# A hybrid decoder layer: three convolutions moved behind the levels of a triangular inverse, and one step of each level moved from VectorE to ScalarE

## The chip, the cores and the metric
One core of a Trainium2 chip runs one launch of the kernel. The metric is the device time in microseconds (us). The engines are TensorE (PE, with its weight loads as PEld), VectorE (DVE), ScalarE (ACT), GpSimd (POOL) and the DMA queues, issued here by SyncE and POOL. Each engine works through its own instructions in order and waits on semaphores for the others.

## The reference
One layer of a decoder trunk over 256 prompt tokens and 8 sample tokens (T = 264 columns), model width 2048, float32. After an RMSNorm one input projection feeds three groups of heads: A (HGRN2 recurrence, 4 heads), B (gated DeltaNet, 8 heads of 128) and C (RG-LRU, 512 channels). An output projection, a SwiGLU feed-forward of width 5632, and norms and residuals follow. What the change touches is group B:

```python
qkv, buf_b_new = causal_dwconv(concat([bq, bk, bv]), buf_b, b_conv_w, None)   # y = w[0]*x[0:L] + w[1]*x[1:] + w[2]*x[2:] + w[3]*x[3:]
qb, kb, vb = split(silu(qkv), 3)
...
A = where(strict, beta_t * (k_t . k_s) * gam, 0)                # per head and chunk of tokens
sol = triangular_solve(eye + A, rhs, lower=True, unit_diagonal=True)
```

## The kernel before
**Chunks and rounds.** All weights stream through four slots as chunks of 512 rows by 256 columns. ACT's `split` rounds a chunk into `w_hi`, DVE's `lo` computes the rest into `w_lo`, and PE's `chunk` multiplies both parts with both parts of the activations, 24 matmuls in all, in two halves of 12. The seven projection rounds (four of kind "b", two of kind "a", one of kind "c") have 16 positions of one chunk each. At position `pos` ACT splits, and DVE makes the rest of, the chunk three positions ahead.

**The mixer beside the stream.** While round r multiplies, each engine also works on the heads projected in round r-1: after each half-chunk PE runs a piece of `b_step` (it counts half positions, `hp` = 2·pos or 2·pos+1), and after its part of the chunk each other engine runs its `b_step(pos)`. So the mixer of B runs in rounds 1 to 4; round 4 itself projects heads of A. The order on each engine is the order of the code; no planner decides it.

**The inverse by levels.** `b_step` inverts I+A by doubling block sizes. The levels l = 2 to 5 run at pos 6 to 9, l = pos-4. Each has two PE products:
- x(l), at hp = 2·pos (L827, L836): eight small matmuls into PSUM bank 4. It needs from DVE the transposed inverse so far (`TMc`, or `TM`) and the masked matrix (`AL`) of its level.
- p(l), at hp = 2·pos+1, half a chunk later (L849): four matmuls, YT times XM, into bank 5. It waits for both operands (semaphore "xc").

Between x and p DVE transposes the first half of x's result out of PSUM (L1876, `YT`), and spreads the second half over the block diagonal of `XM`, by one multiplication with `blk` broadcast, 128x512 (L1877). Then DVE masks AT for the next level (`level_mask`, L1793), waits for p, subtracts it (L1882), and transposes the result (L1885) for the x of the next position. At pos 9 the result is spread instead (L1887) and all of it is transposed (L1890). ACT does nothing for these levels; at pos 6 to 9 it scales four tiles of sample states each (`decay_states`), at pos 7 also four copies for the outer products (`stationary`), and at pos 6 a SiLU of the gate branch. x(6) and x(7), at pos 10 and 11 (L832), are copied by ACT.

**The convolutions.** In a "b" round the projections of q, k and v are ready after pos 3, 7 and 11. ACT copies each into `xraw` (at pos 4, 8 and 12), DVE makes the four taps, two tiles each (`convolve`): q in two parts at pos 6 and 7, k at pos 9 and 10, v at pos 12. ACT's SiLU of each (`silu_conv`) stands at pos 7, 11 and 14, and waits for the convolution to be done. One buffer `conv` serves all three. POOL refills the history columns of `xraw` once a convolution has read them.

Of the kernel before, what the change touches and what calls it, by code (L numbers as in the profile page):

```python
# [30 lines left out]
P = 128  # L31
# [16 lines left out]
CONVW = 4  # L48
XW = 3 + L + NB * CONVW
CW = XW - 3  # L50
B_ROUNDS, A_ROUNDS = 4, 2
# [25 lines left out]
def hybrid_layer(nc, x_prompt, x_sample, state_hgrn, state_gdn, state_gdn_conv, state_rglru_h, state_rglru_conv,  # L77
# [5 lines left out]
    with ExitStack() as ctx:  # L83
# [39 lines left out]
        conv = put("conv", [P, 2, CW])  # L123
# [36 lines left out]
        TMc = sqv[:, 512:640].rearrange("p (x t) -> p x t", x=4)  # L160
        TTc = sqv[:, 640:768].rearrange("p (x t) -> p x t", x=4)
        YT = sqv[:, 768:896].rearrange("p (r t) -> p r t", r=4)
        fold = sqv[:, 768:1024].rearrange("p (x t) -> p x t", x=4)
        kq_st = u[:, :, :].rearrange("p a (c i) -> p (a c) i", i=32)

# [435 lines left out]
        def _(pe):  # L601
# [161 lines left out]
            def b_step(hp, n):  # L763
# [53 lines left out]
                if 12 <= hp <= 23:  # L817
# [21 lines left out]
                    else:  # L839

                        if l < LEVELS - 1:
                            pe.wait_ge(mx["xc"], 10 * n + 2 * l - 2)
                        else:
                            pe.wait_ge(mx["xc"], 10 * n + l + 3)
                        if l == 2:
                            pe.wait_ge(mx["at"], 2 * n + 2)
                        for x in range(4):
# [330 lines left out]
        def _(act):  # L1178
# [88 lines left out]
            def silu_conv(n, which, f=ACT.Silu):  # L1267
                act.wait_ge(conv_done, n + 1)
                A(qkv[:, which, :, 0:L], conv[:, :, 0:L], f).then_inc(silu_done, 1)
                A(qkv[:, which, :, L:T], conv[:, :, L + 3:CW:CONVW], f).then_inc(silu_done, 1)  # L1270

            def evac_plain(g, par, which, f):
                acc_ready(g)
                A(qkv[:, which], acc(par), f).then_inc(drained[par], 1)
# [9 lines left out]
            def decay_states(n, i, factor):  # L1284

                for x in range(4 * i, 4 * i + 4):
                    last = A(Ss[:, x, :], Ss[:, x, :], scale=factor[:, x:x + 1])
                last.then_inc(mx["sdec"], 1)

            def b_step(pos, n):  # L1290
                first = isinstance(n, int) and n == 0
# [111 lines left out]
                    A(S[:, :, 0, :], quad(4)[:, 0:2]).then_inc(mx["s1c"], 1)  # L1403
                finish(pos, n)

            def round_(r, kind, prev, mixer, silu_pos=6):

                for pos in range(SLOTS):
                    slot, turn = (pos + AHEAD) % RING, (pos + AHEAD) // RING
                    if not isinstance(r, int) or SLOTS * r + pos + AHEAD >= RING:  # L1410
                        split(4 * r + turn, slot)
                    q = pos // 4
                    if pos in (4, 8, 12):
                        evac_group(r, kind, q - 1)
                    if prev and pos == silu_pos:
                        act.wait_ge(drained[1], 2 * r)
                        A(qkv[:, 3], qkv[:, 3], ACT.Silu).then_inc(g_done, 1)
                    if kind == "a" and pos == silu_pos:
                        act.wait_ge(drained[0], 2 * r + 1)
                        A(qkv[:, 0], qkv[:, 0], ACT.Silu).then_inc(g_done, 1)  # L1420
                    mixer(pos)
                    if kind == "c" and pos in (13, 15):
                        i = (pos - 13) // 2
                        free_qkv(r, i)
                        silu_conv(12 + i, i, ACT.Copy)
                    if kind == "b" and pos in (7, 11, 14):
                        if not isinstance(r, int) or r > 0:

                            act.wait_ge(mx["nrm"], 2 * r)
                            if pos == 14:  # L1430
                                act.wait_ge(mx["us"], 6 * r)
                        silu_conv(3 * r + q - 1, q - 1)
                    if prev and pos == 1:

                        if not isinstance(r, int) or r > 1:
                            act.wait_ge(mx["og"], 2 * r - 2)
                        evac_plain(4 * r - 1, 1, 3, ACT.Copy)
# [33 lines left out]
                    gating_end()  # L1471

            round_(0, "b", False, mixer0)
            round_(1, "b", True, lambda pos: b_step(pos, 0))
            with act.Fori(2, B_ROUNDS) as r:
                round_(r, "b", True, lambda pos: b_step(pos, r - 1))
            round_(4, "a", True, lambda pos: b_step(pos, 3))
            round_(5, "a", True, lambda pos: a_step(pos, 4, 0), 9)
            round_(6, "c", True, lambda pos: a_step(pos, 5, 1), 9)

# [150 lines left out]
        def _(dve):  # L1631
# [137 lines left out]
                    dve.wait_ge(s, n)  # L1769

            def convolve(n, slot, base, bias=None, taps=range(CONVW)):
                if 0 in taps:
                    dve.wait_ge(raw_q, 2 * n + 2)
                    after(silu_done, 2 * n)
                for j in taps:
                    for t in range(2):
                        w = convw[:, slot, t, j:j + 1]
                        x = xraw[:, slot, t, j:j + CW]
                        if j == 0 and bias is not None:
                            ins = tsc(conv[:, t], x, w, bias[:, t:t + 1], mul, add)  # L1780
                        elif j == 0:
                            ins = tsc(conv[:, t], x, w, None, mul)
                        else:
                            ins = stt(conv[:, t], x, w, conv[:, t], mul, add)  # L1784
                    if j < CONVW - 1:
                        link(ins, base)
                    else:
                        ins.then_inc(conv_done, 1)


            def level_mask(l):

                return tt(AL, AT[:, :, :], masks[:, l, :].unsqueeze(1).broadcast_to([P, 4, P]), mul)  # L1793

            def b_step(pos, n):
                up4 = lambda f: pair[:, f, :].unsqueeze(2).broadcast_to([P, 4, P])
# [73 lines left out]
                    tt(oT[:, :, L:T], j2(small[:, 4, :]), j2(small[:, 5, :]), add).then_inc(mx["os"], 1)  # L1870
                if 6 <= pos <= 9:
                    l = pos - 4
                    by_block = blk[:, :].unsqueeze(1).broadcast_to([P, 4, 4]).unsqueeze(3).broadcast_to([P, 4, 4, 32])
                    wide = lambda a: a.unsqueeze(2).broadcast_to([P, 4, 4, 32])
                    dve.wait_ge(mx["x"], 6 * n + l - 1)
                    dve.transpose(YT, ps[:, 4, 0:P]).then_inc(mx["xc"], 1)  # L1876
                    tt(XM.rearrange("p r (x t) -> p r x t", x=4),  # L1877
                       wide(ps[:, 4, P:2 * P].rearrange("p (r t) -> p r t", r=4)), by_block, mul).then_inc(mx["xc"], 1)
                    if l < LEVELS - 2:
                        level_mask(l + 1).then_inc(mx["al"], 1)  # L1880
                    dve.wait_ge(mx["p"], 6 * n + l - 1)
                    tt(TTc, TTc, ps[:, 5, 0:P].rearrange("p (x t) -> p x t", x=4), sub).then_inc(mx["t"], 1)  # L1882
                    dve.wait_ge(mx["t"], 12 * n + 2 * l - 2)
                    if l < LEVELS - 2:
                        dve.transpose(TMc, TTc).then_inc(mx["t"], 1)  # L1885
                    else:
                        tt(TT[:, :, :].rearrange("p x (r t) -> p x r t", r=4), wide(TTc), by_block, mul)\  # L1887
                            .then_inc(mx["tt"], 1)
                        dve.wait_ge(mx["tt"], 4 * n + 4)
                        dve.transpose(TM, TT[:, :, :]).then_inc(mx["t"], 1)  # L1890
# [151 lines left out]
                        .then_inc(mx["os"], 1)  # L2042

            CV = 3

            def round_(r, kind, mixer, fin, before=lambda pos: None):
                for pos in range(SLOTS):
                    if not isinstance(r, int) or SLOTS * r + pos + AHEAD >= RING:
                        lo(SLOTS * r + pos + AHEAD, (pos + AHEAD) % RING)
                    q = pos // 4  # L2050
                    before(pos)
                    if kind == "b" and pos == 12:
                        chained[0] = 2 * CV
                        convolve(3 * r + 2, 0, 3 * CV * r)
                    mixer(pos)
                    if kind == "c" and pos in (12, 14):
                        i = (pos - 12) // 2
                        chained[0] = CV * i
                        convolve(12 + i, i, 12 * CV, params[:, C_BIAS + 2 * i:C_BIAS + 2 * i + 2])
                    if kind == "b" and pos in (6, 7, 9, 10):  # L2060
                        if pos in (6, 9):
                            chained[0] = CV * (q - 1)
                        convolve(3 * r + q - 1, q - 1, 3 * CV * r,
                                 taps=range(0, 2) if pos in (6, 9) else range(2, CONVW))
                    if pos == 15 and fin is not None:
                        finish(*fin)

# [23 lines left out]

            dve.wait_ge(st_act, 12)
            dve.wait_ge(st_dve, 34)
            round_(1, "b", lambda pos: b_step(pos, 0), (0, 4, B_NORM))
            with dve.Fori(2, B_ROUNDS) as r:
                round_(r, "b", lambda pos: b_step(pos, r - 1), (r - 1, 2 * r + 2, B_NORM))
            round_(4, "a", lambda pos: b_step(pos, 3), (3, 10, B_NORM))
            round_(5, "a", lambda pos: a_step(pos, 4, 0), (4, 0, A_NORM))
            round_(6, "c", lambda pos: a_step(pos, 5, 1), (5, 2, A_NORM))

# [228 lines left out]
```

## Time and profile before
| | |
|---|---|
| median of 3 runs | 1389.5 us (1389.03 to 1390.3) |
| the profiled execution | 1389.01 us, span 1387.3 us |
| PE busy | 1360.2 us, 98% of the span |
| DVE busy | 843.9 us, 61% |
| ACT busy | 678.7 us, 49% |
| mean granted TensorE clock | 0.997 |

Busy time is the union of an engine's instructions. The 1.7 us between the profiled time and the span lie around the first and last instruction. The seven projection rounds lie between about 37 and 500 us of the span, and those with the mixer of B between about 87 and 372 us. The granted clock is a share of full speed.

### The profile page before, as it was taken

What the parts mean: (1) busy time and instruction counts of PE and PEld (TensorE: products, weight loads), DVE (VectorE), ACT (ScalarE), POOL (GpSimd) and SP (SyncE); (2) the same over time, 40 slices, a digit from 0 to 9 for tenths busy, and PEclk for the clock granted to TensorE, in tenths of its full rate; (3) what the DMA queues carried; (4) which work ended last, traced back from release to release, by engine and by line L of the source; (5) the groups of instructions that cost most, each with busy time, mean ns of one, the idle gap of its engine ahead of it and who ended that gap; (6) DMA issues with size and microseconds to landing.
All of it is one profiled execution on the core that took longest, in us unless ns stands there. A gap on an engine that the chain in (4) does not pass through costs nothing.

```text
span 1387.3 us, 28222 instructions
## 1 busy us (share of the span) xinstructions
PE 1360.2 (98%) x11459; PEld 1322.4 (95%) x11459; DVE 843.9 (61%) x1210; ACT 678.7 (49%) x948; POOL 72.2 (5%) x154
## 2 busy tenths in 40 slices
PE   9998989899999999999999999999999999999998
PEld 6997979798999999999999999999999999999998
DVE  5678777878597976476555555555555544444443
ACT  6454646556575685465444444444444434443333
POOL 4010201010201010200000000000000000000000
PEclk9999999999999999999999999999999999999999
DMA  6463635455466446645655555555655555555552
GB/s 211 134 180 95 198 111 152 135 150 165 150 183 194 145 148 205 187 133 160 206 179 182 177 181 179 181 180 181 181 181 181 181 180 180 179 180 180 182 182 79
DMA packets 225255, 234.10 MB, mean 169 GB/s; under 512 B 10443, under 2 KB 220526, under 8 KB 224900
## 3 DMA queue, kind: packets, MB, share of 16 engines
q1 hardware_dynamic: 220500, 218.86, 51.1%
q0 software_dynamic: 4672, 14.04, 3.5%
q8 instruction: 63, 1.03, 0.3%
q14 instruction: 20, 0.16, 0.0%
HBM read 223.45 MB, written 9.65 MB: 168 GB/s over the span
## 4 chain that ended last, share of the span: by engine, by line
PE 87%; DVE 7%; ACT 3%; issue 2%; DMA 1%; SPq 0%; ACTq 0%; POOL 0%; DVEq 0%
PE ps L641 26%; PE ps L642 26%; PE ps L643 26%; DVE w_lo L1638 2%; DVE conv L1784 1%; ACT w_hi L1180 1%; PE ps L941 1%; PE ps L760 1%; DMA xtok<-in_x_prompt_dram 1%; PE ps L770 1%; PE ps L1129 1%; PE ps L667 0%; DVE rs L1877 0%; PE ps L796 0%; PE ps L849 0%
## 5 line engine op out<-in xcount | busy, mean ns | idle before, releaser
L1638 DVE TENSOR_TENSOR w_lo<-raw,w_hi 128x1024 fp32r<-128x1024 f32 x408 | 499.7, 1227 | 434.8 <-ACT w_hi L1180 433.0
L1180 ACT ACTIVATE w_hi<-raw 128x1024 fp32r<-128x1024 f32 x408 | 431.0, 1059 | 554.5 <-PE ps L643 549.0
L641 PE MATMUL ps<-act_hi,w_hi 128*128 128x264 f32 x2296 | 665.6, 290 | 0.7 <-DVE act_lo L1652 0.4
L642 PE MATMUL ps<-act_lo,w_hi 128*128 128x264 f32 x2296 | 652.4, 284 | 0.0
L643 PE MATMUL ps<-act_hi,w_lo 128*128 128x264 f32 x2296 | 651.5, 284 | 0.0
L641 PEld LDWEIGHTS ps<-act_hi,w_hi 128*128 128x128 f32 x2296 | 433.1, 189 | 8.7 <-issue 6.1
L642 PEld LDWEIGHTS ps<-act_lo,w_hi 128*128 128x128 f32 x2296 | 433.6, 189 | 1.2
L643 PEld LDWEIGHTS ps<-act_hi,w_lo 128*128 128x128 f32 x2296 | 432.3, 188 | 0.0
L642 PE MATMUL ps<-hid_lo,w_hi 128*128 128x264 f32 x696 | 197.8, 284 | 0.0
L641 PE MATMUL ps<-hid_hi,w_hi 128*128 128x264 f32 x696 | 197.7, 284 | 0.0
L643 PE MATMUL ps<-hid_hi,w_lo 128*128 128x264 f32 x696 | 197.6, 284 | 0.0
L641 PEld LDWEIGHTS ps<-hid_hi,w_hi 128*128 128x128 f32 x696 | 131.1, 188 | 0.0
L642 PEld LDWEIGHTS ps<-hid_lo,w_hi 128*128 128x128 f32 x696 | 130.9, 188 | 0.0
L643 PEld LDWEIGHTS ps<-hid_hi,w_lo 128*128 128x128 f32 x696 | 130.8, 188 | 0.0
L641 PE MATMUL ps<-cat_hi,w_hi 128*128 128x264 f32 x248 | 70.9, 286 | 0.0
L643 PE MATMUL ps<-cat_hi,w_lo 128*128 128x264 f32 x248 | 70.3, 284 | 0.0
L642 PE MATMUL ps<-cat_lo,w_hi 128*128 128x264 f32 x248 | 70.3, 283 | 0.0
L642 PEld LDWEIGHTS ps<-cat_lo,w_hi 128*128 128x128 f32 x248 | 46.7, 188 | 0.1
L641 PEld LDWEIGHTS ps<-cat_hi,w_hi 128*128 128x128 f32 x248 | 46.7, 188 | 0.1
L643 PEld LDWEIGHTS ps<-cat_hi,w_lo 128*128 128x128 f32 x248 | 46.6, 188 | 0.0
L1784 DVE SCALAR_TENSOR_TENSOR conv<-xraw,convw,conv 128x288 f32<-128x288 f32 x84 | 39.7, 514 | 1.2
L535 POOL DMA_DIRECT2D out_dram<-Ss x12 | 10.7, 894 | 250.0 <-DVE S L2038 100.2
(386 smaller groups left out, 1064.6 us busy)
## 6 DMA issues: line engine op xcount, KB each, us to landing
raw<-in_w_in_dram SPq DMA_DIRECT2D x112, 512.0 KB, 3.7
raw<-in_w_gate_dram SPq DMA_DIRECT2D x88, 512.0 KB, 3.5
raw<-in_w_up_dram SPq DMA_DIRECT2D x88, 512.0 KB, 3.5
raw<-in_w_down_dram SPq DMA_DIRECT2D x88, 512.0 KB, 4.4
raw<-in_w_out_dram SPq DMA_DIRECT2D x32, 512.0 KB, 3.5
out_dram<-Ss POOLq DMA_DIRECT2D x12, 512.0 KB, 5.2
Ss<-in_state_gdn_dram POOLq DMA_DIRECT2D x8, 512.0 KB, 6.6
xtok<-in_x_prompt_dram SPq DMA_DIRECT2D x2, 1024.0 KB, 6.0
```

The costliest lines, as they stand in the source:

```text
L535: pool.dma_start(dst_s[0, :, ds(2 * k + j, 1)].rearrange("b o d e -> d (b o) e"), Ss[:, 8 * j:8 * j + 8, :]).then_inc(mx["st"], 16)
L641: pe.matmul(out, wh, x_hi[:, kk], start=(kk == begin), stop=False)
L642: pe.matmul(out, wh, x_lo[:, kk], start=False, stop=False)
L643: last = pe.matmul(out, wl, x_hi[:, kk], start=False, stop=(kk == nk - 1))
L760: pe.matmul(ps[:, 7 - a * (g % 2), :], k_st[a][:, g, :], u_mv[a][:, :, :], start=True, stop=True)\
L770: last = pe.matmul(ps[:, 4 + i, 0:T], ones[:, :], sq[:, i], start=True, stop=True)
L941: last = pe.matmul(ps[:, 4 + l // 4, (l % 4) * P:(l % 4) * P + P], w, w, start=True, stop=True)
L1129: ins = pe.matmul(ps[:, Y_BANKS[q][t], k * P:k * P + P], src[:, 4 * q + k, t * P:t * P + P], ident, is_transpose=True, start=(first and k ...
L1180: return act.activation(out, in_, f, **kw)
L1638: tt(w_lo[:, slot], raw[:, slot], w_hi[:, slot].bitcast(F32), sub).then_inc(lo_done, 1)
L1784: ins = stt(conv[:, t], x, w, conv[:, t], mul, add)
```

## The change
1. DVE's two steps between x(l) and p(l) at pos 6 to 9 are replaced. ACT copies the first half of x's result to SBUF (`Yc`), and spreads the second half by four copies of 128x128, each scaled by one column of `blk`. DVE transposes `YT` out of `Yc`.
2. Both parts are called by `ahead(pos)`, first thing at a position: ahead of ACT's `split` and DVE's `lo` of the chunk three ahead. Before, DVE's part came behind its `lo`.
3. The first tap of the three convolutions of a "b" round goes to ACT (`first_tap`: two scaled copies of 128x288), at pos 4 for q, and behind the SiLU of the one before it at pos 11 and 12 for k and v.
4. DVE's other three taps go to pos 10, 11 and 12, one convolution each. ACT's SiLUs go to pos 11, 12 and 14.
5. Semaphore counts follow: "xc" counts three steps per level, `raw_q` three per convolution of B. The convolutions of C keep their four taps on DVE.

```diff
 # TensorE
-  pe.wait_ge(mx["xc"], 10 * n + 2 * l - 2)
+  pe.wait_ge(mx["xc"], 14 * n + 3 * l - 3)
 # ScalarE
+            def first_tap(n, slot):
+                act.wait_ge(raw_q, 3 * n + 2)
+                if not isinstance(n, int) or n > 0:
+                    act.wait_ge(silu_done, 2 * n)
+                for t in range(2):
+                    last = A(conv[:, t], xraw[:, slot, t, 0:CW], scale=convw[:, slot, t, 0:1])
+                last.then_inc(raw_q, 1)
...
+            def b_answer(pos, n):
+                if 6 <= pos <= 9:
+                    if pos == 6:
+                        act.wait_ge(mx["ks"], n + 1)
+                    act.wait_ge(mx["x"], 6 * n + pos - 5)
+                    A(Yc, ps[:, 4, 0:P]).then_inc(mx["xc"], 1)
+                    for x in range(4):
+                        last = A(XM[:, :, 32 * x:32 * x + 32], ps[:, 4, P:2 * P].rearrange("p (r t) -> p r t", r=4),
+                                 scale=blk[:, x:x + 1])
+                    last.then_inc(mx["xc"], 1)
...
                 for pos in range(SLOTS):
+                    ahead(pos)
                     slot, turn = (pos + AHEAD) % RING, (pos + AHEAD) // RING
...
-                    if kind == "b" and pos in (7, 11, 14):
+                    if kind == "b" and pos == 4:
+                        first_tap(3 * r, 0)
+                    if kind == "b" and pos in (11, 12, 14):
+                        i = (11, 12, 14).index(pos)
...
-                        silu_conv(3 * r + q - 1, q - 1)
+                        silu_conv(3 * r + i, i)
+                        if i < 2:
+                            first_tap(3 * r + i + 1, (i + 1) % 2)
 # VectorE
+            def b_answer(pos, n):
+                if 6 <= pos <= 9:
+                    dve.wait_ge(mx["xc"], 14 * n + 3 * pos - 17)
+                    dve.transpose(YT, Yc).then_inc(mx["xc"], 1)
...
                 if 6 <= pos <= 9:
                     l = pos - 4
-                    dve.wait_ge(mx["x"], 6 * n + l - 1)
-                    dve.transpose(YT, ps[:, 4, 0:P]).then_inc(mx["xc"], 1)
-                    tt(XM.rearrange("p r (x t) -> p r x t", x=4),
-                       wide(ps[:, 4, P:2 * P].rearrange("p (r t) -> p r t", r=4)), by_block, mul).then_inc(mx["xc"], 1)
                     if l < LEVELS - 2:
+                        dve.wait_ge(mx["x"], 6 * n + l - 1)
                         level_mask(l + 1).then_inc(mx["al"], 1)
...
                 for pos in range(SLOTS):
+                    ahead(pos)
                     if not isinstance(r, int) or SLOTS * r + pos + AHEAD >= RING:
                         lo(SLOTS * r + pos + AHEAD, (pos + AHEAD) % RING)
                     q = pos // 4
                     before(pos)
-                    if kind == "b" and pos == 12:
-                        chained[0] = 2 * CV
-                        convolve(3 * r + 2, 0, 3 * CV * r)
                     mixer(pos)
...
-                    if kind == "b" and pos in (6, 7, 9, 10):
-                        if pos in (6, 9):
-                            chained[0] = CV * (q - 1)
-                        convolve(3 * r + q - 1, q - 1, 3 * CV * r,
-                                 taps=range(0, 2) if pos in (6, 9) else range(2, CONVW))
+                    if kind == "b" and pos in (10, 11, 12):
+                        i = pos - 10
+                        chained[0] = TAPS * i
+                        convolve(3 * r + i, i % 2, 3 * TAPS * r, taps=range(1, CONVW))
```

## Rows read from the trace of the kernel before
**Rows 1.** TensorE's waits: line, released by, us in total, times, longest.
```profile
PE ps L849 <- DVE rs L1877: 13.2, 10, 2.9
PE ps L985 <- DVE gz L1684: 1.2, 1, 1.2
```
**Rows 2.** Timeline of TensorE, round 4: start us, us, engine, line, operation, count.
```profile
333.02 0.43 PE L827 MATMUL ps<-sq 128*32 128x128 f32 x8
333.26 0.40 PE L836 MATMUL ps<-masks,sq 128*32 128x128 f32 x8
...
342.62 0.43 PE L827 MATMUL ps<-sq 128*32 128x128 f32 x8
...
345.07 0.43 PE L849 MATMUL ps<-rs,sq 128*32 128x128 f32 x8
347.09 0.43 PE L827 MATMUL ps<-sq 128*32 128x128 f32 x8
...
351.86 0.44 PE L832 MATMUL ps<-rs,AT 32*32 32x32 f32 x16 [0.23 <-DVE rs L1890]
```
**Rows 3.** Timeline of TensorE, round 1.
```profile
111.96 0.42 PE L827 MATMUL ps<-sq 128*32 128x128 f32 x8
...
127.37 0.66 PE L849 MATMUL ps<-rs,sq 128*32 128x128 f32 x8 [2.93 <-DVE rs L1877]
130.82 0.42 PE L827 MATMUL ps<-sq 128*32 128x128 f32 x8
...
135.59 0.44 PE L832 MATMUL ps<-rs,AT 32*32 32x32 f32 x16 [0.23 <-DVE rs L1890]
```
**Rows 4.** Busy time in one us of round 1; PEclk is the granted clock.
```profile
128.00:129.00 1.00, 1.00 (x8) 1.00 (x5) 0.87 (x3) 1.00 (x4) 0.00 (x0) 0.50 0.82 240
```
**Rows 5.** Timeline of TensorE, round 3.
```profile
260.30 0.43 PE L827 MATMUL ps<-sq 128*32 128x128 f32 x8
...
282.52 0.44 PE L832 MATMUL ps<-rs,AT 32*32 32x32 f32 x16 [0.23 <-DVE rs L1890]
```
**Rows 6.** Timeline of ScalarE, round 2, pos 7.
```profile
197.73 0.75 ACT L1180 ACTIVATE qkv<-conv 128x512 f32<-128x512 f32 x2 [3.05 <-DVE conv L1784]
```
**Rows 7.** Timeline of VectorE, round 2, pos 8.
```profile
199.46 1.22 DVE L1638 TENSOR_TENSOR w_lo<-raw,w_hi 128x1024 fp32r<-128x1024 f32 x1 [1.76 <-ACT w_hi L1180]
200.60 0.31 DVE L1876 STREAM_TRANSPOSE sq<-ps 128x128 f32<-128x128 f32 x1
...
201.41 0.67 DVE L1793 TENSOR_TENSOR sq<-AT,masks 128x512 f32<-128x512 f32 x1
202.04 0.29 DVE L1882 TENSOR_TENSOR sq<-sq,ps 128x128 f32<-128x128 f32 x1
202.36 0.31 DVE L1885 STREAM_TRANSPOSE sq<-sq 128x128 f32<-128x128 f32 x1
```
**Rows 8.** Timeline of ScalarE, round 4, pos 6 and 7.
```profile
332.15 1.28 ACT L1180 ACT_TABLE_LOAD   x1
333.44 1.18 ACT L1180 ACTIVATE qkv<-qkv 128x528 f32<-128x528 f32 x2
...
335.70 1.04 ACT L1180 ACTIVATE w_hi<-raw 128x1024 fp32r<-128x1024 f32 x1
339.26 1.14 ACT L1180 ACTIVATE kst_b<-ps,group 128x128 fp32r<-128x128 f32 x4 [2.52 <-PE ps L749]
340.27 1.28 ACT L1180 ACTIVATE Ss<-Ss,spair 128x128 f32<-128x128 f32 x4
```
**Rows 9.** Timeline of VectorE, round 4, pos 9.
```profile
350.36 0.69 DVE L1887 TENSOR_TENSOR TT<-sq,blk 128x512 f32<-128x512 f32 x1
351.09 0.71 DVE L1890 STREAM_TRANSPOSE rs<-TT 128x512 f32<-128x512 f32 x1
```
**Rows 10.** Round 3, pos 12: TensorE, then VectorE.
```profile
291.82 0.60 PE L871 MATMUL ps<-vb,TT 128*128 128x128 f32 x4
...
293.20 2.92 DVE L1784 SCALAR_TENSOR_TENSOR conv<-xraw,convw,conv 128x288 f32<-128x288 f32 x6
```

More of the change, by code:

```diff
@@ L162, in hybrid_layer @@
         YT = sqv[:, 768:896].rearrange("p (r t) -> p r t", r=4)
+        Yc = sqv[:, 896:1024]
         fold = sqv[:, 768:1024].rearrange("p (x t) -> p x t", x=4)
@@ L841, in b_step @@
                         if l < LEVELS - 1:
-                            pe.wait_ge(mx["xc"], 10 * n + 2 * l - 2)
+                            pe.wait_ge(mx["xc"], 14 * n + 3 * l - 3)
                         else:
-                            pe.wait_ge(mx["xc"], 10 * n + l + 3)
+                            pe.wait_ge(mx["xc"], 14 * n + l + 7)
                         if l == 2:
@@ L1404, in a_step, with round_ @@
                 finish(pos, n)
-            def round_(r, kind, prev, mixer, silu_pos=6):
+            def round_(r, kind, prev, mixer, silu_pos=6, ahead=lambda pos: None):
                 for pos in range(SLOTS):
+                    ahead(pos)
                     slot, turn = (pos + AHEAD) % RING, (pos + AHEAD) // RING
@@ L1425, in round_ @@
                         silu_conv(12 + i, i, ACT.Copy)
-                    if kind == "b" and pos in (7, 11, 14):
+                    if kind == "b" and pos == 4:
+                        first_tap(3 * r, 0)
+                    if kind == "b" and pos in (11, 12, 14):
+                        i = (11, 12, 14).index(pos)
                         if not isinstance(r, int) or r > 0:
                             act.wait_ge(mx["nrm"], 2 * r)
-                            if pos == 14:
+                            if i == 2:
                                 act.wait_ge(mx["us"], 6 * r)
-                        silu_conv(3 * r + q - 1, q - 1)
+                        silu_conv(3 * r + i, i)
+                        if i < 2:
+                            first_tap(3 * r + i + 1, (i + 1) % 2)
                     if prev and pos == 1:
@@ L1473, in _ @@
             round_(0, "b", False, mixer0)
-            round_(1, "b", True, lambda pos: b_step(pos, 0))
+            round_(1, "b", True, lambda pos: b_step(pos, 0), ahead=lambda pos: b_answer(pos, 0))
             with act.Fori(2, B_ROUNDS) as r:
-                round_(r, "b", True, lambda pos: b_step(pos, r - 1))
-            round_(4, "a", True, lambda pos: b_step(pos, 3))
+                round_(r, "b", True, lambda pos: b_step(pos, r - 1), ahead=lambda pos: b_answer(pos, r - 1))
+            round_(4, "a", True, lambda pos: b_step(pos, 3), ahead=lambda pos: b_answer(pos, 3))
             round_(5, "a", True, lambda pos: a_step(pos, 4, 0), 9)
@@ L1771, in convolve @@
             def convolve(n, slot, base, bias=None, taps=range(CONVW)):
-                if 0 in taps:
-                    dve.wait_ge(raw_q, 2 * n + 2)
-                    after(silu_done, 2 * n)
+                if bias is None:
+                    dve.wait_ge(raw_q, 3 * n + 3)
+                else:
+                    dve.wait_ge(raw_q, 2 * n + 2 + 3 * B_ROUNDS)
+                    dve.wait_ge(silu_done, 2 * n)
                 for j in taps:
@@ L1778, in convolve @@
                         x = xraw[:, slot, t, j:j + CW]
-                        if j == 0 and bias is not None:
+                        if j == 0:
                             ins = tsc(conv[:, t], x, w, bias[:, t:t + 1], mul, add)
-                        elif j == 0:
-                            ins = tsc(conv[:, t], x, w, None, mul)
                         else:
@@ L1793, in level_mask, with wide @@
                 return tt(AL, AT[:, :, :], masks[:, l, :].unsqueeze(1).broadcast_to([P, 4, P]), mul)
+            by_block = blk[:, :].unsqueeze(1).broadcast_to([P, 4, 4]).unsqueeze(3).broadcast_to([P, 4, 4, 32])
+            def wide(a):
+                return a.unsqueeze(2).broadcast_to([P, 4, 4, 32])
+            def b_answer(pos, n):
+                if 6 <= pos <= 9:
+                    dve.wait_ge(mx["xc"], 14 * n + 3 * pos - 17)
+                    dve.transpose(YT, Yc).then_inc(mx["xc"], 1)
             def b_step(pos, n):
@@ L1872, in b_step @@
                     l = pos - 4
-                    by_block = blk[:, :].unsqueeze(1).broadcast_to([P, 4, 4]).unsqueeze(3).broadcast_to([P, 4, 4, 32])
-                    wide = lambda a: a.unsqueeze(2).broadcast_to([P, 4, 4, 32])
-                    dve.wait_ge(mx["x"], 6 * n + l - 1)
-                    dve.transpose(YT, ps[:, 4, 0:P]).then_inc(mx["xc"], 1)
-                    tt(XM.rearrange("p r (x t) -> p r x t", x=4),
-                       wide(ps[:, 4, P:2 * P].rearrange("p (r t) -> p r t", r=4)), by_block, mul).then_inc(mx["xc"], 1)
                     if l < LEVELS - 2:
+                        dve.wait_ge(mx["x"], 6 * n + l - 1)
                         level_mask(l + 1).then_inc(mx["al"], 1)
@@ L2044, in _, with round_ @@
             CV = 3
-            def round_(r, kind, mixer, fin, before=lambda pos: None):
+            TAPS = 2
+            def round_(r, kind, mixer, fin, before=lambda pos: None, ahead=lambda pos: None):
                 for pos in range(SLOTS):
+                    ahead(pos)
                     if not isinstance(r, int) or SLOTS * r + pos + AHEAD >= RING:
@@ L2058, in round_ @@
                         chained[0] = CV * i
-                        convolve(12 + i, i, 12 * CV, params[:, C_BIAS + 2 * i:C_BIAS + 2 * i + 2])
-                    if kind == "b" and pos in (6, 7, 9, 10):
-                        if pos in (6, 9):
-                            chained[0] = CV * (q - 1)
-                        convolve(3 * r + q - 1, q - 1, 3 * CV * r,
-                                 taps=range(0, 2) if pos in (6, 9) else range(2, CONVW))
+                        convolve(12 + i, i, 3 * B_ROUNDS * TAPS, params[:, C_BIAS + 2 * i:C_BIAS + 2 * i + 2])
+                    if kind == "b" and pos in (10, 11, 12):
+                        i = pos - 10
+                        chained[0] = TAPS * i
+                        convolve(3 * r + i, i % 2, 3 * TAPS * r, taps=range(1, CONVW))
                     if pos == 15 and fin is not None:
@@ L2093, in _ @@
             dve.wait_ge(st_dve, 34)
-            round_(1, "b", lambda pos: b_step(pos, 0), (0, 4, B_NORM))
+            round_(1, "b", lambda pos: b_step(pos, 0), (0, 4, B_NORM), ahead=lambda pos: b_answer(pos, 0))
             with dve.Fori(2, B_ROUNDS) as r:
-                round_(r, "b", lambda pos: b_step(pos, r - 1), (r - 1, 2 * r + 2, B_NORM))
-            round_(4, "a", lambda pos: b_step(pos, 3), (3, 10, B_NORM))
+                round_(r, "b", lambda pos: b_step(pos, r - 1), (r - 1, 2 * r + 2, B_NORM),
+                       ahead=lambda pos: b_answer(pos, r - 1))
+            round_(4, "a", lambda pos: b_step(pos, 3), (3, 10, B_NORM), ahead=lambda pos: b_answer(pos, 3))
             round_(5, "a", lambda pos: a_step(pos, 4, 0), (4, 0, A_NORM))
```

## The prediction, made before the result was known
> **What bounds the kernel now.** I read the busy shares first: PE works 98% of the span, so a change that takes nothing from PE can win only PE's idle time, some 27 us, and PE's stretches at a low clock. The view of waits comes second. It says who ends that idle time [rows 1]: 13.2 us in ten waits, all of them p(l) waiting for DVE's spreading multiplication, and one of 1.2 us in round 0 for the small tables at pos 12. Third comes the timeline, to see what stands in front of the late multiplication. In round 2 the long one (2.9 us) is a chain over two engines. ACT's SiLU at pos 7 waits 3.05 us for the first convolution [rows 6], the split of pos 8 is queued behind the SiLU, DVE sits 1.76 us until that split is done [rows 7], and only behind its `lo` may it answer x(4). Rounds 1 and 3 have the same; round 4, without convolutions, has not.
>
> A measure that holds all these waits is the time from x(2), at pos 6, to x(6), at pos 10. It is 18.84 us in round 4 [rows 2], 23.63 in round 1 [rows 3], 22.22 in round 3 [rows 5]; round 2 repeats round 1 with 23.70. Sum 88.39 us. Where PE isn't held it does a position in 4.47 us (342.62 to 347.09 [rows 2]), and the last one in 4.77 - 0.23 = 4.54, so PE's own pace would be about 3 x 4.47 + 4.54 = 17.95.
>
> The extra of round 1 has a second part. Behind the 2.93 us of idle time the granted clock is 0.50, the lower of the two levels, 1.2 GHz [rows 4], and p(4) to x(5) takes 3.45 us [rows 3] where the same work took 2.02 in round 4 [rows 2]. That costs 1.43 us. Round 2 repeats it; round 3 has a wait as long and keeps its clock.
>
> **The new loop.** The answers themselves come in time. x lasts 0.64 us (333.02 to 333.66 [rows 2]). ACT starts some 0.04 later and issues five instructions. The nearest row is `stationary`: four scaled 128x128 copies out of PSUM, 1.01 us from the first's start to the next group's [rows 8], 0.25 each. So the split can start at 0.68 + 1.26 = 1.94 us after x's start, and XM is done 0.13 later, at 2.07. PE reaches p at about 2.0 at pos 6 and 2.45 at pos 7 to 9 (342.62 to 345.07 [rows 2]; there the outer products stand between). The 13.2 us of waits in front of p are gone, but for 0.1 at pos 6.
>
> What is late next? The next x needs DVE's mask, subtraction and transposition, and in DVE's queue they stand behind `lo`, which needs ACT's split, which now stands behind the answers, which need this x. That closes a loop from x to x, which PE can't run ahead of:
> - x ends and ACT starts: 0.68
> - five copies: 1.26, so 1.94
> - split: 1.04 [rows 8], 2.98; DVE's `lo` starts at 3.01
> - `lo` to the next DVE instruction: 1.14 [rows 7], 4.15
> - mask: 0.63, 4.78; subtraction: 0.32, 5.10; transposition: 0.31, 5.41 [rows 7]
> - PE starts the next x 0.06 later: 5.47.
>
> (The p that the subtraction needs ended at 2.5 to 2.9.) At pos 9 there is no mask; subtraction 0.32, spreading 0.73 (350.36 to 351.09), transposition 0.71 [rows 9] give 4.15 + 1.76 + 0.06 = 5.97. From x(2) to x(6): 3 x 5.47 + 5.97 = 22.38 us. PE is held 1.0 us in front of x at pos 8 and 9, and 1.4 at pos 7 and 10.
>
> Is ACT back in time? At pos 6 of rounds 1 to 3, after the split: table load 1.29, then a SiLU and four decays, 2.26 less one SiLU of 0.54 (333.44 to 335.70 [rows 8]), so free at 2.98 + 0.02 + 1.29 + 1.72 = 6.01, against 6.15 when the next x ends. In round 4 there are two SiLUs: 6.55, 0.4 late, so 22.78. At the other positions ACT has over 0.9 us to spare.
>
> **The sum.** Round 1: 22.38 - 23.63 = -1.25. Round 2: -1.32. Round 3: +0.16. Round 4: 22.78 - 18.84 = +3.94. In these the convolutions' stalls and both stretches of low clock are already taken out.
>
> **The convolutions.** In round 0 less stands ahead of the small tables: DVE has spent six tap instructions there (2.92 us [rows 10]) instead of sixteen, and the wait of 1.2 [rows 1] goes: -1.2. In rounds 1 to 3 I put the convolutions' new places at nothing. The first starts about 4.6 us after x(6), when DVE has updated states, and ends at 7.5; `lo` and the subtraction of p(7) follow and end at 9.1, and PE wants that at 9.30 (282.52 to 291.82 [rows 5, 10]). The cover there is only 0.2 us. The second runs from 9.6 to 12.5 and the third from 14.0 to 17.0. Each has six tap instructions of 2.92 in all. The `lo` between them are for chunks that PE starts after 21. On ACT a SiLU and a first tap (no row has its shape; it lies between a 128-column copy, 0.25, and a 528-column one, 0.54, twice; I take 0.75) stand ahead of the copies of u, which then start at 10.8 instead of 10.4, with PE coming for them at 11.6. The first tap at pos 4 falls where ACT idles. POOL's refill follows the first convolution, in time for the copy of v at about 10. If a cover fails, it costs 0.2 to 0.5 us in each of three rounds; if the work in front goes quicker than I think, nothing is won, as PE is not waiting there. Raw loads hang on `lo`, which is four positions ahead of its need.
>
> **Total:** -1.2 - 1.25 - 1.32 + 0.16 + 3.94 = +0.3 us on the profiled execution's 1389.01. The median shown is 0.5 above that one, so I forecast 1389.8.
>
> **The unknown prices.** The five copies are on the loop, sixteen times. Their lower end is the 0.25 above. The upper end is the four decay copies, out of SBUF: 1.28 wide against 1.14 [rows 8], 0.05 more apiece. That gives 16 x 5 x 0.05 = +3.8, 1393.6. I take 0.25, since source and scale are those of `stationary`. The other price is the clock: nothing to win, and at most 1.43 a round.
>
> The Trainium skill, "ScalarE: Activation LUTs", section "Rules for kernel authors", budgets about 0.3 us for an ACTIVATE plus 0.83 ns for each element, and sends multiplications to VectorE. An estimate by it is 0.41 us a copy, 2.0 us for an answer, and some +13 us in all. The trace doesn't agree: four such copies are through in 1.14 us [rows 8]. I leave that rule at a chance of 2%.
>
> **Rivals.**
> 1. *The waits go and nothing takes their place* (10%). For it: all the PE waits that the profile names are for the removed instruction. Against it: two queues in fixed order. Then each round runs at 17.95: 88.39 - 71.8 = 16.6, and 1.2 of round 0: 1371.
> 2. *The clock falls in every round* (18%), at pos 7 to 10, each time PE is held for 1 to 1.4 us. It decides from the point where such short idle times, four in a row, are enough; the rows show a fall only behind 2.9 us, and not behind the 1.2 in round 0. Price: 4 x 1.43 = +5.7, 1395.5. Slower. The Trainium skill, "TensorE: Matmul & The Clock Gate", section "A second HAM failure mode: psum-queue depth-cycling", says that frequent short idles between groups of matmuls can make the clock swing. No row here shows such a swing behind a short idle.
> 3. *The copies are dearer than `stationary`'s* (15%), by the SBUF price: 1393.6. Slower.
> 4. *Half the loop isn't there* (9%), say because ACT's instructions overlap better or PE's first wait is shorter: 0.5 us less in each of the 16 beats minus what PE itself needs, some -5: 1384.
> 5. *The covers of pos 11 and 12 fail* (5%): 3 x 0.5, 1391.3.
>
> The forecast, with its own range 1388 to 1392, has the remaining 41%, after 2% for the rule on ScalarE.
>
> **How the numbers follow.** The range of 1384.5 to 1396 leaves out rival 1, part of rival 4, and the skill's rule. A measurement of this kernel can tell 0.2%, 2.8 us, from no change. Faster by more than that (below 1386.7): rivals 1 and 4 and a little of the forecast, 0.21. Slower (above 1392.3): rivals 2 and 3, the rule, and a tail of the forecast, 0.35. Within: 0.44.
>
> **What would show it.** In the profile after: no wait of L849 over 0.2 us; a new group of PE waits at the first matmuls of x, released by DVE's transpositions, of 1.0 to 1.5 us, about 16 of them; x to x of 5.5 us at pos 6 to 8, and 6.0 from pos 9; on DVE, `lo` at pos 6 to 9 released by ACT's w_hi each time; round 4 longer from x(2) to x(6) by 4 us, rounds 1 and 2 shorter by 1.3; granted clock 1.00 throughout them; the wait in round 0 gone. I am wrong if x starts at PE's own pace of 4.5 us a position (then 1371), or if the clock shows 0.50 in round 4.

## The result and the profile after

The changed kernel takes 1393.78 us (median of 8 runs, 1393.42 to 1395.07) against 1389.14 for the kernel before (8 runs, 1387.54 to 1390.45). The ratio is 1.0034, 95% interval 1.0023 to 1.0045: slower by 4.6 us. The profiled execution took 1393.59 us, its span is 1391.8, 4.5 more than before. Times here and below are medians; one execution of the second experiment's kernel took 3298.8 us at a full granted clock, against 1375.23 to 1375.42 in its other three, and no run shows why.

TensorE's waits after, in the columns of [rows 1]:

```profile
PE ps L828 <- DVE sq L1918: 13.3, 12, 1.3
PE ps L833 <- DVE rs L1923: 5.6, 4, 1.4
...
PE ps L642 <- DVE xT L1725: 0.9, 1, 0.9
```

The waits in front of p (L849 before, L850 here) are gone, and the one for the small tables too. In their place stand twelve waits in front of x(3), x(4) and x(5) (L828) and four in front of x(6) (L833), 18.9 us where there were 13.2 in front of p and 0.9 in front of x(6), all released by DVE's transpositions. (The third row is PE at the start of round 1, waiting for DVE's copy of the residual out of PSUM.) Round 4 on TensorE, which answers to [rows 2]:

```profile
332.19 0.42 PE L828 MATMUL ps<-sq 128*32 128x128 f32 x8
...
337.77 0.43 PE L828 MATMUL ps<-sq 128*32 128x128 f32 x8 [1.27 <-DVE sq L1918]
...
343.55 0.43 PE L828 MATMUL ps<-sq 128*32 128x128 f32 x8 [1.31 <-DVE sq L1918]
...
349.06 0.43 PE L828 MATMUL ps<-sq 128*32 128x128 f32 x8 [0.98 <-DVE sq L1918]
...
355.00 0.44 PE L833 MATMUL ps<-rs,AT 32*32 32x32 f32 x16 [1.39 <-DVE rs L1923]
...
361.07 0.68 PE L833 MATMUL ps<-rs,AT 64*64 64x64 f32 x8
```

And one turn of the loop, from the x at 343.55, first on ScalarE, then on VectorE (to be held against [rows 7, 8]):

```profile
344.25 0.28 ACT L1181 ACTIVATE sq<-ps 128x128 f32<-128x128 f32 x1 [1.06 <-PE ps L837]
344.43 1.14 ACT L1181 ACTIVATE rs<-ps,blk 128x128 f32<-128x128 f32 x4
345.43 1.08 ACT L1181 ACTIVATE w_hi<-raw 128x1024 fp32r<-128x1024 f32 x1
```
```profile
346.55 1.23 DVE L1665 TENSOR_TENSOR w_lo<-raw,w_hi 128x1024 fp32r<-128x1024 f32 x1 [1.67 <-ACT w_hi L1181]
347.69 0.69 DVE L1820 TENSOR_TENSOR sq<-AT,masks 128x512 f32<-128x512 f32 x1
348.29 0.28 DVE L1915 TENSOR_TENSOR sq<-sq,ps 128x128 f32<-128x128 f32 x1
348.61 0.31 DVE L1918 STREAM_TRANSPOSE sq<-sq 128x128 f32<-128x128 f32 x1
```

The reader can follow it by start times: ACT's answers, the split queued behind them, DVE idle until the split is done, then `lo`, mask, subtraction, transposition, and PE's next x at 349.06, 5.51 us after the last.

A second thing shows only in the windows. Busy time and granted clock (third number from the end) behind the wait at pos 10, in rounds 3 and 4:

```profile
282.00:283.00 1.00, 1.00 (x6) 1.00 (x6) 0.00 (x0) 0.00 (x0) 0.00 (x0) 0.50 0.33 27
357.00:358.00 1.00, 1.00 (x7) 1.00 (x6) 0.00 (x0) 0.00 (x0) 0.00 (x0) 0.50 0.37 41
```

The two low stretches of rounds 1 and 2 [rows 4] have gone, and two came in rounds 3 and 4. x(6) to x(7) takes 6.07 us in round 4 above (355.00 to 361.07), 6.09 in round 3, and 4.65 in rounds 1 and 2: some 1.4 us more each. Yet in rounds 1 and 2 PE waits in front of x(6) just as long (1.41 and 1.39 us) and its granted clock stays at 1.00. Round 1:

```profile
133.65 0.44 PE L833 MATMUL ps<-rs,AT 32*32 32x32 f32 x16 [1.41 <-DVE rs L1923]
...
138.30 0.68 PE L833 MATMUL ps<-rs,AT 64*64 64x64 f32 x8
```

The whole difference of the spans by stretches (x(2) to x(6) from the starts of x, rows as above in each round):

| stretch | before | after | difference |
|---|---|---|---|
| to x(2) of round 1 | 111.96 | 111.11 | -0.85 |
| round 1, x(2) to x(6) | 23.63 | 22.54 | -1.09 |
| round 2 | 23.70 | 22.48 | -1.22 |
| round 3 | 22.22 | 22.49 | +0.27 |
| round 4 | 18.84 | 22.81 | +3.97 |
| between rounds 1, 2 and 3 | 101.01 | 101.42 | +0.41 |
| round 3, x(6), to round 4, x(2) | 50.50 | 52.15 | +1.65 |
| behind x(6) of round 4 | 1035.44 | 1036.80 | +1.36 |
| sum | 1387.3 | 1391.8 | +4.5 |

### The profile page after: what moved, and what is told of

Its sections match the earlier page's. It is cut to its first block, busy times and chain, and to the rows that moved or that the text cites. A ratio compares the mean times of both kernels' runs of the same rounds, so it can differ in the third digit from the quotient of the medians.

```text
span 1391.8 us, 28299 instructions
## 1 busy us (share of the span) xinstructions
PE 1360.7 (98%) x11459; PEld 1323.2 (95%) x11459; DVE 827.8 (59%) x1170; ACT 707.5 (51%) x1051; POOL 74.7 (5%) x154
## 4 chain that ended last, share of the span: by engine, by line
PE 87%; DVE 6%; ACT 5%; issue 2%; DMA 1%; SPq 0%; ACTq 0%; DVEq 0%
PE ps L642 26%; PE ps L643 26%; PE ps L644 26%; ACT w_hi L1181 2%; DVE w_lo L1665 2%; ACT rs L1181 1%; PE ps L942 1%; DVE conv L1811 1%; PE ps L771 1%; DVE sq L1820 1%; DMA xtok<-in_x_prompt_dram 1%; PE ps L1130 1%; PE ps L828 0%; PE ps L668 0%; PE ps L761 0%
## 5 line engine op out<-in xcount | busy, mean ns | idle before, releaser
L514 POOL COPY xraw<-hist_b 128x24 f32<-128x24 f32 (+1 forms) x24 | 11.1, 461 | 216.2 <-DVE conv L1811 197.4
```

Source lines behind the costliest of these rows:

```text
L514: pool.tensor_copy(dst[:, :, 0:3], src).then_inc(hist_in, 1)
```

## The experiments

All were run beside the kernel before, which took 1390.05 us beside kernels 1 to 4, 1390.01 beside 5 to 8 and 1389.37 beside 9. Ratios are against it.

**1. Both engines' order turned back.** The question is whether the order closes the loop.

```diff
 # ScalarE, round_
-                    ahead(pos)
                     slot, turn = ...
                         split(4 * r + turn, slot)
+                    ahead(pos)
 # VectorE, round_
-                    ahead(pos)
                         lo(SLOTS * r + pos + AHEAD, (pos + AHEAD) % RING)
+                    ahead(pos)
```

> The changed kernel, but ACT's split and DVE's w_lo of the chunk three ahead stand in front of the answers again. Theory (a loop from x to x through answers, split and w_lo of the same position): the loop opens, x(2) to x(6) falls from 22.5 to 22.8 us to about 18.5 in each of four rounds (some wait of up to 1.4 us stays in front of p at pos 7, where ACT is late by the table load, SiLU and split), the clock stays at 1.00, and the time is 1393.8 - 16.3 - 2.9 = 1374.6 us. Rival (ACT's added load itself is what holds PE, 5 copies a level wherever they stand): x to x stays at 5.5 us and the time within 2 us of 1393.8.

Measured: 1376.67 us (1376.43 to 1377.11), ratio 0.9906 (0.9889 to 0.9922). x(2) to x(6) takes 18.9 us in rounds 1 to 3 and 19.5 in round 4, and no low clock shows in these rounds. That is 2.1 us more than expected: PE still waits in front of p, eight times and 4.0 us in all, for DVE's transposition, which stands behind `lo`. The same instructions in another order are 17.1 us faster than the changed kernel, so ACT's added load isn't what holds PE.

**2. Only ACT's order turned.** The first half of the diff above.

> The changed kernel, only ACT's order turned: split first, then the answers; DVE still transposes before its w_lo. Theory: the split is the one link that closes the loop, so this is as good as both turned, 1374.6 us, within 1 us. Rival (DVE's order matters too): only part of the gain, 1380 or more.

Measured: 1375.33 us, ratio 0.9895 (0.9875 to 0.9914). The split's place on ACT is the link. It is even 1.3 us better than both turned. DVE in round 4, from x(2) at 318.99, shows why the `lo` is harmless now:

```profile
320.09 0.30 DVE L1831 STREAM_TRANSPOSE sq<-sq 128x128 f32<-128x128 f32 x1
320.32 1.18 DVE L1665 TENSOR_TENSOR w_lo<-raw,w_hi 128x1024 fp32r<-128x1024 f32 x1
321.43 0.68 DVE L1820 TENSOR_TENSOR sq<-AT,masks 128x512 f32<-128x512 f32 x1
```

It starts right behind the transposition, 1.33 us after x, with nothing to wait for. What is left is one wait a round, at pos 7, in front of p(3), and ACT shows its cause in round 4:

```profile
321.10 1.28 ACT L1181 ACT_TABLE_LOAD   x1
322.39 1.18 ACT L1181 ACTIVATE qkv<-qkv 128x528 f32<-128x528 f32 x2
323.48 1.27 ACT L1181 ACTIVATE Ss<-Ss,spair 128x128 f32<-128x128 f32 x4
324.64 1.05 ACT L1181 ACTIVATE w_hi<-raw 128x1024 fp32r<-128x1024 f32 x1
325.59 0.26 ACT L1181 ACTIVATE sq<-ps 128x128 f32<-128x128 f32 x1
```
```profile
326.92 0.43 PE L850 MATMUL ps<-rs,sq 128*32 128x128 f32 x8 [1.22 <-ACT rs L1181]
```

**3. Only DVE's order turned.** The second half of the diff.

> The changed kernel, only DVE's order turned: w_lo first, then the transposition of Yc. Theory: DVE's w_lo waits for ACT's split, which waits for x, so YT comes at x + 4.4 us instead of x + 1.3, p waits 2 us for it, and x to x becomes 6.5 us (6.75 from pos 9): 26.2 us from x(2) to x(6), +3.7 a round, 1408.5 us. Rival (the DVE order is harmless): 1394.

Measured: 1411.78 us, ratio 1.016 (1.0143 to 1.0177). x to x is 6.5 us, as expected, and 6.8 from pos 9, but 8.0 from x(2) to x(3); a round takes 27.9. PE waits in front of p now, and DVE of round 2 shows the transposition behind a `lo` that itself waits:

```profile
PE ps L850 <- DVE sq L1831: 32.8, 16, 2.3
```
```profile
201.10 1.22 DVE L1665 TENSOR_TENSOR w_lo<-raw,w_hi 128x1024 fp32r<-128x1024 f32 x1 [5.18 <-ACT w_hi L1181]
202.25 0.30 DVE L1831 STREAM_TRANSPOSE sq<-sq 128x128 f32<-128x128 f32 x1
```

The 1.5 us too many from x(2) to x(3) are low clock. It falls in each of the four rounds behind the first wait in front of p, of 2.20 to 2.26 us, and not behind the twelve waits of 1.95 to 2.03 us that follow. TensorE in round 2, and the granted clock (third number from the end) behind its first and its second wait:

```profile
194.58 0.66 PE L850 MATMUL ps<-rs,sq 128*32 128x128 f32 x8 [2.20 <-DVE sq L1831]
198.10 0.43 PE L828 MATMUL ps<-sq 128*32 128x128 f32 x8
202.60 0.42 PE L850 MATMUL ps<-rs,sq 128*32 128x128 f32 x8 [2.02 <-DVE sq L1831]
```
```profile
195.00:196.00 1.00, 1.00 (x11) 0.83 (x5) 0.70 (x3) 1.00 (x5) 0.00 (x0) 0.50 0.44 55
203.00:204.00 1.00, 1.00 (x12) 1.00 (x9) 0.96 (x4) 0.26 (x1) 0.00 (x0) 1.00 0.44 56
```

That makes four falls where the changed kernel has two, and 1408.5 plus two more of 1.5 us is 1411.5. While ACT answers first, DVE's place for the transposition is worth 18 us; with ACT's split in front (1, 2) it is worth 1.3. So the change's `ahead` on DVE is right; the one on ACT is wrong.

**4. The convolutions' half alone.** Two steps of DVE between x and p as in the kernel before (L1876, L1877), no answers on ACT; first taps, convolutions and SiLUs as in the change; the semaphore counts follow.

```diff
-                        dve.wait_ge(mx["x"], 6 * n + l - 1)
+                    dve.wait_ge(mx["x"], 6 * n + l - 1)
+                    dve.transpose(YT, ps[:, 4, 0:P]).then_inc(mx["xc"], 1)
+                    tt(XM..., wide(ps[:, 4, P:2 * P]...), by_block, mul).then_inc(mx["xc"], 1)
```

> The convolution half of the change alone: first taps on ACT, convolutions at pos 10 to 12, SiLUs at pos 11, 12 and 14; the spreading stays one multiplication on DVE, behind w_lo, as in the kernel before. Theory: the long stall at pos 8 goes, rounds 1 to 3 look like round 4 did before (18.84 us from x(2) to x(6)), no fall of the clock: 1389.1 - 13.0 - 0.85 + 0.4 = 1375.7 us. Rival (the convolutions' new places cost something at pos 10 to 12, or the stall isn't from them): above 1380.

Measured: 1376.04 us, ratio 0.99 (0.9883 to 0.9916). x(2) to x(6) is 18.84 to 18.86 us in all four rounds, exactly what round 4 had before. One wait a round is left in front of p(2), 0.9 us. DVE of round 4 has two `lo` to do before it may answer x(2):

```profile
PE ps L850 <- DVE rs L1897: 3.6, 4, 0.9
```
```profile
320.22 2.35 DVE L1654 TENSOR_TENSOR w_lo<-raw,w_hi 128x1024 fp32r<-128x1024 f32 x2
322.49 0.31 DVE L1896 STREAM_TRANSPOSE sq<-ps 128x128 f32<-128x128 f32 x1
322.72 0.65 DVE L1897 TENSOR_TENSOR rs<-ps,blk 128x512 f32<-128x512 f32 x1
```

**5. The answers' half alone.** All taps on DVE at their old places, SiLUs at pos 7, 11 and 14; `ahead` as in the change.

```diff
-                    if kind == "b" and pos == 4:
-                        first_tap(3 * r, 0)
-                    if kind == "b" and pos in (11, 12, 14):
+                    if kind == "b" and pos in (7, 11, 14):
...
-                    if kind == "b" and pos in (10, 11, 12):
...
+                    if kind == "b" and pos in (6, 7, 9, 10):
...
```

> The other half of the change alone: ACT's answers in front of everything at pos 6 to 9, the convolutions with all taps on DVE at their old places, SiLUs at pos 7, 11 and 14. Theory (the loop of 5.5 us, plus the convolution's stall once a round: the SiLU at pos 7 waits for the convolution until some 2.4 us after the next x, and the answer is queued behind it): x(2) to x(6) of about 24.9 us in rounds 1 to 3 and 22.8 in round 4, so 1389.1 + (97.5 - 88.4) - (2.9 of old low clock already within) = 1398 to 1402 us. Rival (the answers are a gain that the moved convolutions spoil): below 1389.

Measured: 1400.22 us, ratio 1.0071 (1.0054 to 1.0088). x(2) to x(6): 24.91, 24.71, 24.73 and 22.83. Its waits are the loop's, plus three in front of p:

```profile
PE ps L828 <- DVE sq L1913: 13.1, 11, 1.4
PE ps L833 <- DVE rs L1918: 5.6, 4, 1.4
PE ps L850 <- ACT rs L1181: 5.4, 3, 1.8
```

Here too each round has a wait of 1.41 or 1.42 us in front of x(6), and the clock falls behind it in rounds 1 and 4 and not in 2 and 3. It also falls once behind a wait of 1.83 us in front of p(4) in round 1, and not behind those of 1.78 and 1.77 in rounds 2 and 3.

By itself one half is worth -14.0 us (4) and the other +10.2 (5); together they should give -3.8 and gave +4.6. They don't add: without the answers, moving the convolutions wins 14.0 us, and with them (5 against the changed kernel) 6.4, because the loop then holds PE anyway.

**6. A dose on the loop.** The decays, 1.17 us of ACT, between answers and split.

```diff
                                  scale=blk[:, x:x + 1])
                     last.then_inc(mx["xc"], 1)
...
+                    decay_states(n, pos - 6, spair[:, 0, :])
...
-                if 6 <= pos <= 9:
...
-                    decay_states(n, pos - 6, spair[:, 0, :])
```

> The changed kernel, with ACT's four decays of sample states (1.17 us) between the answers and the split instead of behind it: the same work, put on the loop. Theory: each x to x at pos 6 to 9 grows by 1.17, 16 of them, 18.7 us, less 0.4 in round 4 where ACT was late anyway: 1412 us. Rival (ACT's load counts, not its place): 1394.

Measured: 1412.84 us, 19.1 above the changed kernel; ratio 1.0162 (1.0145 to 1.0179). PE's waits in front of x grow from 18.9 to 31.0 us:

```profile
PE ps L828 <- DVE sq L1916: 22.8, 12, 2.4
PE ps L833 <- DVE rs L1921: 8.2, 4, 2.6
```

This is 12.1 us more, and less than the 18.3 expected, because the low clock shows in every round here and lengthens PE's own part of a turn (mean granted clock 0.99). Turns without low clock show the dose by itself: in round 2 x(4) to x(5) grows from 5.51 to 6.67 us and x(5) to x(6) from 5.94 to 7.10, 1.16 each. The whole of x(2) to x(6) grows by 20.8 us in the four rounds, with the low clock in it.

**7 and 8. Which wait brings the clock down?** First the wait in front of x(6) alone is taken away, by the split in front of the answers at pos 9; then it alone is left.

```diff
-                    ahead(pos)
+                    if pos != 9:
+                        ahead(pos)
...
                         split(4 * r + turn, slot)
+                    if pos == 9:
+                        ahead(pos)
```

(The eighth kernel has `pos == 9` and `pos != 9` exchanged.)

> The changed kernel, with the split in front of the answers at pos 9 alone. It takes PE's last and longest wait of each round (1.4 us, in front of x(6)) and leaves the three before. x(5) to x(6) falls from 5.94 to 4.77: 4.7 us less. Theory A of the clock (it fell behind that longest wait): granted clock 1.00 in all rounds, 2.9 us more, 1386.2 us. Theory B (it falls from the row of waits): two low stretches remain, 1389.1 us.

> The opposite: the split in front of the answers at pos 6, 7 and 8, behind them at pos 9 alone, so that one wait of 1.4 us stands in each round by itself. x(2) to x(6) is that of both engines' or ACT's order turned (18.6, round 4 19.2) plus 1.17: 1375.3 + 4.7 = 1380.0 us if a single such wait leaves the clock alone; up to 5.8 more if it brings it down (theory A).

Measured: 1386.07 us (7 runs), ratio 0.9973 (0.9962 to 0.9985), and 1384.34 us (5 runs), ratio 0.9959 (0.9944 to 0.9973). x(5) to x(6) is 4.77 in the one and 5.95 in the other. The stretch behind pos 9 of the first, and behind pos 9 in rounds 1 and 2 of the second:

```profile
132.00:137.00 5.00, 4.64 (x68) 4.09 (x67) 3.50 (x7) 1.60 (x3) 0.00 (x0) 1.00 0.56 169
```
```profile
133.00:134.00 1.00, 1.00 (x6) 1.00 (x5) 0.00 (x0) 0.00 (x0) 0.00 (x0) 0.50 0.33 30
...
204.00:205.00 1.00, 1.00 (x7) 1.00 (x6) 0.23 (x1) 0.00 (x0) 0.00 (x0) 0.50 0.09 31
```

With twelve waits of 0.96 to 1.31 us and only 0.2 in front of x(6) there is no low clock between 60 and 400 us in the profiled execution. With 1.41 us in front of x(6) in each round, and 0.6 to 1.2 in front of p(3) as in the second kernel, it falls in all four rounds, and x(6) to x(7) is 6.06 to 6.12 each time. The second kernel has those waits in front of p(3) too and no low clock, so it is the wait in front of x(6) that brings it down here: theory A, for these two kernels. The median is 4.3 us above 1380.0. The profiled execution, with four falls, is the slowest, 5.2 above (mean clock 0.994); the fastest, 1382.88, has 0.997. The number of falls seems to vary from one execution to the next, but only the profiled one has a trace. Of the seventh kernel's executions one took 1387.49 us at 0.998, the others 1385.88 to 1386.25 at 0.999 to 1.000; that looks like one fall. Nor does theory A say when such a wait does it: the changed kernel and the fifth have it in all rounds, and the clock falls behind it in two of four.

**9. The last wait of the second experiment.** ACT's order is turned as there, and the SiLU of the gate branch moves.

```diff
-            def round_(r, kind, prev, mixer, silu_pos=6, ahead=lambda pos: None):
+            def round_(r, kind, prev, mixer, silu_pos=10, ahead=lambda pos: None):
```

> ACT's order turned (split, then answers, as in the best one so far at 1375.3 us), and the SiLU of the gate branch in rounds 1 to 4, with its table load, moved from pos 6 to pos 10. What was left there was one wait of PE a round in front of p(3) at pos 7, 0.6 to 1.2 us, where ACT was late by table load, SiLU, decays and split. Theory: that wait goes, x(2) to x(6) falls from 18.6 (19.2 in round 4) to about 18.0, no fall of the clock: 1375.3 - 3.2 = 1372.1 us, unless the SiLU costs as much at pos 10 (rival: 1375).

Measured: 1372.02 us (1371.97 to 1372.62), ratio 0.9875 (0.9859 to 0.9891), the fastest of all, 21.8 us below the changed kernel. x(2) to x(6) is 17.88 in each round, PE's own pace. Of the waits in front of x and p only this one is left, 0.2 us a round:

```profile
PE ps L833 <- DVE rs L1923: 0.9, 4, 0.2
```

## Why the prediction was right, and where it was off

- **The loop** was right, link by link. x to x was forecast at 5.47 and is 5.50 to 5.58 (5.78 once, in round 4, where ACT is late by table load and two SiLUs; 0.3 us more, 0.4 forecast); 5.97 from pos 9 was forecast and is 5.94. A round was forecast at 22.38 and 22.78, and is 22.5 and 22.81. The turned order (1, 2) and the dose (6) show that it is this loop, and that its link is the split.
- **The copies' price** was right: 1.14 us for four. Rival 3 is out: ACT's answer and split together start to end in 2.26 us (344.25 to 346.51), against 2.30 forecast.
- **The answers come in time for p**: right, no wait in front of p is left.
- **The clock** is the term that was mis-sized. I took 2.9 us of low clock out of rounds 1 and 2 and put none back. In the profiled execution 1.42 and 1.44 us came back, behind the wait of 1.39 in front of x(6) in rounds 4 and 3. The prediction named "the clock shows 0.50 in round 4" as a sign of being wrong, and it does show it: on this term it was wrong. Rival 2 had the price right (1.43) and the count and the trigger not: two rounds instead of four, and no row of short idles is needed, as the eighth kernel shows. I had taken the 1.2 us in round 0 as a sign that such a wait does nothing; it was too thin a base. The Trainium skill, "TensorE: Matmul & The Clock Gate", section "A second HAM failure mode: psum-queue depth-cycling", says that frequent short idles between groups of matmuls can make the clock swing. The traces agree in part: in the eighth kernel the clock fell behind waits of 1.41 us, one a round, and in the seventh it kept 1.00 through three of 0.96 to 1.31 a round.
- **Round 0** was forecast at -1.2 and gave -0.85. The wait for the tables went, but three convolutions (2.91 us each, from 66.04 to 79.11) now stand in front of DVE's copies of the residual there, and PE waits 0.89 us at the start of round 1 (0.28 before).
- **The covers at pos 10 to 12** held. The rest of a round costs 0.2 us more, three times. The fourth kernel, with the same convolutions, confirms that their new places are nearly free: 14.0 us won.
- Together: 0.33 (the forecast's sum) + 0.35 (round 0) + 0.40 (the loop) + 0.62 (between rounds) + 2.86 (clock) - 0.06 (behind x(6) of round 4) = 4.5, which is the difference of the spans.
- **The total.** 1389.8 was forecast and 1393.78 measured. Without the clock it would lie in the forecast's own range, 1388 to 1392; it lies only in the wide one. The likeliest outcome, within 0.2% of no change, had 0.44 and did not come; "slower", with 0.35 (which is rivals 2 and 3 and the rule alone, with nothing left for the tail of the forecast named there), did. That the result lies 0.2 us from rival 3's 1393.6 is chance, as the copies cost what was forecast.
- **Rival 1** (1371, nothing takes the waits' place) was wrong for this change, and is near what the ninth kernel reaches by another order: 17.88 us a round (17.95 forecast) and 1372.0 in all.

What stays open is when a wait brings the clock down. Its length doesn't decide it: 1.41 us in front of x(6) do in four rounds of the eighth kernel and in two of four in the changed one and the fifth; in the third 2.20 us do and three of 1.95 to 2.03 don't. Nor do only the sixteen matmuls of 32x32 of x(6), since the third kernel's falls come in front of p. The loop's 22.5 us a round, on the other hand, are the same in rounds with and without a fall.

## What to carry to other kernels

When a step that waits for an engine is moved in front of a step that feeds the same engine's next item, look for the loop: the sum of everything from one item to the next, over all queues. Here 1 us of split that had slack stood inside it after the move; 13.2 us of waits went and 18.0 new ones came. Put the work whose inputs are already there in front, and the answer behind it, if the answer then still starts on time: so with the split on ACT. Where that work may itself be late, the answer goes first: so with `lo` on DVE as long as the split is late. And test the two halves of a change alone: here one was worth 14 us, and the other undid it.

## What the runs showed of the hardware

- A granted clock of 0.50 behind a wait of PE of only 1.41 us, in all four rounds of the eighth kernel's profiled execution, at 1.42 to 1.48 us apiece. A wait as long (1.39 to 1.42) had it in two of four rounds in the changed kernel and in the fifth. Three waits of 0.96 to 1.31 us within 17 us, in each round of the seventh, had none, nor had the twelve of 1.95 to 2.03 us in the third.
- The spread of the kernel before goes with the clock: of its 11 runs beside kernels 5 to 8 the fastest, 1387.56 us, has a mean granted clock of 0.999, the two slowest, 1391.78 and 1392.13, have 0.994. Where their low stretches lie is not shown. The kernels that have no wait of 1.2 us or more in front of x and p (1, 4, 9) lie within 0.7 us, at 0.998 to 1.000.
